# Moving four weight buffers by 128 bytes inside on-chip memory

## The reference, cut to what matters

```
proj = h @ w_in[l]
gates = jax.nn.sigmoid((h @ w_gate[l]).reshape(B, S, N_BRANCHES, D) + b_gate[l])
mixed = jnp.sum(gates * up, axis=2) @ w_out[l]
m = jnp.square(jax.nn.relu(h @ w_up[l])) @ w_down[l]
...
p = h @ w_l
return (g_a * y_a + g_b * y_b) @ w_o
```

## Time and profile before

| What | Value |
|---|---|
| median of three runs | 2254.39 us |
| profiled execution | 2254.39 us |
| its span | 2252.6 us |
| TensorE busy | 2216.8 us, 98% |
| VectorE busy | 1510.1 us, 67% |
| ScalarE busy | 1071.6 us, 48% |
| GpSimd busy | 121.5 us, 5% |
| granted TensorE clock, mean | 0.996 |
| HBM read | 468.09 MB, 210 GB/s over the span |

### The profile page before, as it was taken

The page is one execution under the profiler, slowest core; times in us unless marked ns, Lnnn a source line. Parts: engine busy times, 40 slices in busy tenths (PEclk is TensorE's granted clock), DMA queues, the critical chain, the costliest instruction groups (busy, mean ns, idle before and its releaser), DMA issues.

```text
span 2252.6 us, 37367 instructions
## 1 busy us (share of the span) xinstructions
PE 2216.8 (98%) x15836; PEld 2065.2 (92%) x15836; DVE 1510.1 (67%) x1864; ACT 1071.6 (48%) x1422; POOL 121.5 (5%) x81
## 2 busy tenths in 40 slices
PE   7999999999999999999999999999999999999998
PEld 7889999999999888988988998998889989999986
DVE  6867588899989767554555554555766555678655
ACT  5444435554444456544443443444656545444443
POOL 1100010111100201000000000000100000011000
PEclk9999999999999999999999999999999999999999
DMA  8855667677787665656656656656754545788763
GB/s 279 240 179 163 201 211 247 218 237 254 240 267 245 236 227 178 191 196 191 196 193 195 192 194 196 201 194 204 246 173 147 157 135 165 245 295 292 254 215 139
DMA packets 246382, 474.73 MB, mean 211 GB/s; under 512 B 21054, under 2 KB 25512, under 8 KB 244424
## 3 DMA queue, kind: packets, MB, share of 16 engines
q1 hardware_dynamic: 242888, 454.40, 63.0%
q0 software_dynamic: 3328, 17.96, 2.3%
HBM read 468.09 MB, written 4.21 MB: 210 GB/s over the span
## 4 chain that ended last, share of the span: by engine, by line
PE 90%; DVE 6%; issue 1%; ACT 1%; POOL 1%; DMA 1%; POOLq 0%; SPq 0%; ACTq 0%; DVEq 0%
PE ps L867 18%; PE ps L869 18%; PE ps L868 18%; PE ps L860 11%; PE ps L862 11%; PE ps L861 11%; DVE wloW L1227 1%; DVE tmp L1255 1%; PE ps L795 1%; DVE tmp L1400 1%; PE ps L651 1%; PE ps L677 1%; ACT whiW L899 1%; POOL tmp L538 0%; PE ps L784 0%
## 5 line engine op out<-in xcount | busy, mean ns | idle before, releaser
L867 PE MATMUL ps<-op0h,whiW 128*128 128x256 f32 x3248 | 907.4, 279 | 7.7 <-DVE wloW L1227 7.7
L869 PE MATMUL ps<-op0h,wloW 128*128 128x256 f32 x3248 | 899.3, 277 | 0.0
L868 PE MATMUL ps<-op0l,whiW 128*128 128x256 f32 x3248 | 899.3, 277 | 0.0
L1227 DVE TENSOR_TENSOR wloW<-raw,whiW 128x1024 fp32r<-128x1024 f32 (+1 forms) x488 | 600.2, 1242 | 339.5 <-ACT whiW L899 337.2
L899 ACT ACTIVATE whiW<-raw 128x1024 fp32r<-128x1024 f32 (+1 forms) x488 | 512.3, 1057 | 569.6 <-PE ps L869 421.6
L867 PEld LDWEIGHTS ps<-op0h,whiW 128*128 128x128 f32 x3248 | 612.1, 188 | 11.5 <-DVE wloW L1227 7.0
L868 PEld LDWEIGHTS ps<-op0l,whiW 128*128 128x128 f32 x3248 | 612.3, 189 | 2.0 <-issue 1.4
L869 PEld LDWEIGHTS ps<-op0h,wloW 128*128 128x128 f32 x3248 | 612.2, 188 | 0.0
L1227 DVE TENSOR_TENSOR wloT<-raw,whiT 128x1024 fp32r<-128x1024 f32 (+1 forms) x280 | 338.3, 1218 | 274.3 <-ACT whiT L899 274.0
L899 ACT ACTIVATE whiT<-raw 128x1024 fp32r<-128x1024 f32 (+1 forms) x280 | 290.8, 1047 | 318.1 <-PE ps L862 257.6
L860 PE MATMUL ps<-whiT,op1h 128*128 128x512 f32 x640 | 249.4, 390 | 0.0
(11 more groups left out here) (260 smaller groups left out, 2178.1 us busy)
## 6 DMA issues: line engine op xcount, KB each, us to landing
raw<-in_w_in SPq DMA_DIRECT2D x256, 512.0 KB, 4.4
raw<-in_w_up SPq DMA_DIRECT2D x128, 512.0 KB, 3.8
raw<-in_w_down SPq DMA_DIRECT2D x128, 512.0 KB, 4.0
raw<-in_w_ada SPq DMA_DIRECT2D x96, 512.0 KB, 5.0
raw<-in_w_gate SPq DMA_DIRECT2D x96, 512.0 KB, 4.9
raw<-in_w_out SPq DMA_DIRECT2D x64, 512.0 KB, 4.4
raw<-in_w_branch SPq DMA_DIRECT2D x48, 512.0 KB, 5.2
raw<-in_w_proj_a SPq DMA_DIRECT2D x24, 512.0 KB, 5.0
```

Of the source, the lines that this page charges most:

```text
L867: pe.matmul(o, wh, xh[:, ka, :], start=first and m % 2 == 0, stop=False, skip_group_check=True)
L868: pe.matmul(o, wh, xl[:, ka, :], start=False, stop=False, skip_group_check=True)
L869: mm = pe.matmul(o, wl, xh[:, ka, :], start=False, stop=last, skip_group_check=True)
L1227: v.tensor_tensor(wlo[job.mode][q % NSPL][:, :, 0:job.n], x, h.bitcast(F32), ALU.subtract).then_inc(s_lo, 1)
```

## The change

`split_buffers` had a second argument, the distance in bytes from a slot's start to its W buffer: 64 for the high parts and 192 for the low parts. It now has none, and 64 holds for both.

```diff
-        def split_buffers(name, stand):
+        def split_buffers(name):
 ...
-                for mode, shift in (("T", 0), ("W", stand)):
+                for mode, shift in (("T", 0), ("W", 64)):
                     w[mode].append(at(f"{name}{mode}{i}", [128, KC, 512], o + shift, F32R))
-                top[0] = o + stand + 4 * KC * 512
+                top[0] = o + 64 + 4 * KC * 512
             return w
 
-        whi, wlo = split_buffers("whi", 64), split_buffers("wlo", 192)
+        whi, wlo = split_buffers("whi"), split_buffers("wlo")
```

## The result

The changed kernel took 2285.2 us, the median of four runs (2280.08 to 2289.41 us), against 2254.52 us for the kernel before (four runs, 2254.38 to 2257.48 us). The recorded ratio of the runs is 1.0132, with a 95% interval of 1.0108 to 1.0155. I had forecast 2254.4 us.

A forecast was written before the change was run, and what follows sets the result against it. The prediction took the kernel to be bound by the pace at which TensorE's matmuls follow one another. Its terms, 2254.39 + 0 + 0 + 0, gave 2254.4 us, with an 8-in-10 range of 2250.3 to 2258.5 us.

The forecast's parts named there:

- The weight loads: Term for TensorE's load of `wloW` in mode W: pace independent of start address, 0 us, bounds -15.2 to +16.3 us.
- Mode T as a witness: Argument that mode T, standing and moving both at remainder 64, keeps the same pace: 226.7 ns, twice 113.3 for twice the columns.
- Rows 10: Profile rows of mode W's slowest stall-free stretch found, 8 matmuls at 117.5 ns each; gave the upper bound, +16.3 us.
- Rival A: Loads sharing a remainder collide, slowing line 868's matmuls from 113.3 towards 117.5 ns: +16.3 us, 2270.7 us; chance 0.04.
- The writes: Term for VectorE's write of `wloW` (line 1227, mode W): address makes no difference, 0 ns a write.
- Rival D: VectorE's writes of `wloW` slower by the full 13 ns, nothing hiding them: 6.2 us, 2260.6 us; chance 0.02.
- Other meetings: Term for engines' steps meeting at other moments, one TensorE wait for `wloW` more or less: 0, range +-3.1 us.
- Rival B: Remainder 0 of `wloW` costs something now; line 868's pace would go towards 109.4 ns: -15.2 us, 2239.2 us; chance 0.04.

The follow-up runs named there:

- one_in_four: Changed kernel with only the fourth of the four `wloW` buffers back at remainder 0 modulo 256: 2261.3 us.
- write0_load128: Changed kernel with `wloW` written by VectorE at remainder 0 as before, still loaded by TensorE at 128 (wrong columns computed): 2288.9 us.
- both64: Changed kernel with `whiW` and `wloW` both at remainder 64, like the activations, instead of 128: 2320.9 us.
- swap: Kernel before with the two remainders exchanged, `whiW` at 0 and `wloW` at 128: 2264.3 us.
- write128_load0: Changed kernel with `wloW` still written by VectorE at remainder 128, but loaded by TensorE at 0 as before (wrong columns computed): 2253.9 us.
- next_slot: Changed kernel with each chunk's low part in the next of the four slots, both parts still at remainder 128: 2286.6 us.
- lo224: Kernel before with `wloW` at remainder 224 instead of 0, `whiW` still at 128: 2298.6 us.
- lo32: Kernel before with `wloW` at remainder 32 instead of 0, `whiW` still at 128: 2292.2 us.

## Why the prediction was wrong

**The weight loads, the step that failed.** I argued that loads with remainders 128, 0 and 64 all went at 113.3 ns, that the trace held 2 x 3888 loads of the kind that `wloW` was to become, and took 0 us. Each of these numbers was right. What failed is the inference that a load's cost is its own. `one_in_four` shows that the pace is a state of the whole stream, and `write0_load128` that the loads alone decide on it: the loads of `whiW` at 128 were fast because the load of `wloW` at 0 between them kept the 117.8 ns pace from lasting. With it gone, all three lines slowed, not only the third of the stream that I had put at stake (440.5 us) and charged nothing. The three kinds of distance have means of 117.0, 117.0 and 116.8 ns, against 113.5 ns each before, and the term is 39.8 us where I had 0.

**Mode T as a witness** failed as well. Standing and moving at one remainder is the best layout there and the worst in mode W (`both64`, 120.0 ns). A matmul of 256 columns beside a load of 128 is not half of one of 512.

**Rows 10 were the state itself.** I used 117.5 ns as an upper bound and left it an oddity. It was the 117.8 ns pace, already in the trace in rows of up to 8, each time close behind a break in the stream. That something ended it was the thing to explain, and the one candidate that differed from its neighbours was the remainder of `wloW`. Rival A had this pace and the right sign, at a chance of 0.04, but charged it to line 868 alone: 16.3 us. All three lines, slow 80% of the time, give 3 x 16.3 x 0.80 = 39.1 us, close to the 39.8 us measured. Its condition, that loads share a remainder, isn't the right one either: in `swap` they don't, and the slow pace lasted for up to 1,126 matmuls. Nor do writes take part.

**The writes** were right. The write's mean went from 1246 to 1257 ns and its idle time from 336.3 to 354.3 us, and `write128_load0` shows that its address has no effect. Rival D is refuted by the same run. The median stayed at 1225 ns. The mean follows the loads and not the write's own address: it is 1243 ns in `write128_load0` and 1256 ns in `write0_load128`. Why a slower stream lengthens some of the writes isn't shown.

**Other meetings** went the way of fewer stalls, 5.3 us in all, outside my +-3.1 us.

**Rival B** asked whether remainder 0 had a cost. It had a use. Its lower end rested on a row of another kind: the transposes of the earlier trace rows move 128 columns each, so 109.4 ns is no faster stream than 113.3 ns for 256. The Trainium skill ("TensorE: Matmul & The Clock Gate", section "Back-to-back issue gap") gives N/2.4 plus 2.5 ns for isolated warm matmuls, by which an estimate for 256 columns is 109.2 ns. The mean of no layout here came down to that; 113.5 ns was the lowest, wherever the operands lay as a whole.

What stays open: what in the memory makes the two paces, why a stretch starts in one or the other (the stretch near 940 us in the changed kernel started fast, of itself), and whether a third operand layout, say with `op0h` and `op0l` at different remainders, is faster than 113.3 ns. None of these was tried. The start of a stretch may well be a matter of chance: with the loads at the same remainders the changed kernel has 9,250 slow distances, `write0_load128` 8,679 and `next_slot` 8,534, and the changed kernel's four times lie 9.3 us apart where those of the kernel before lie 3.1 us apart.

## What to carry to other kernels

- Where TensorE is the bound and weights are loaded beside every matmul, the start addresses of the moving and standing operands, modulo 256 bytes, are a parameter worth up to 3.8% here (2254.5 to 2339.8 us, both modes together). Write them down as such and measure them, all together: moving all of them by 64 or by 32 bytes changed nothing, moving the low part alone by 32 cost 38 to 44 us.
- A uniform pace in a trace doesn't prove that each instruction's cost is its own. Look for the short stretches with another pace, ask what ends them, and whether the change takes that away.
- Read the pace from starts; the page's busy times and durations showed this loss only as 3 ns.

## What the hardware did that I had not expected

- A stream of float32r matmuls with 256 moving columns can run at two lasting paces, 113.3 and 117.8 ns a matmul, with the same instructions and remainders (in the changed kernel for up to 644 and 1,918 distances in a row); where standing and moving operands have one remainder it runs at 120.0 ns. At 2.4 GHz 256 columns are 106.7 ns, so the 113.3 ns pace is 1/16 and the last 1/8 above one column per cycle. In mode T 226.7 ns are 1/16 above 213.3.
- A single weight load at remainder 0 among loads at 128 can switch the slow pace off until the next break in the stream (20 slow rows in `one_in_four` end with one). The reverse, a load at 128 among loads at 0, doesn't do it (`swap`, slow rows of up to 1,126).
- Where VectorE writes has no part in it (2253.9 and 2288.9 us with the write's place exchanged against the load's).
- A distance of 128 bytes matters and one of 256 more doesn't (2285.2 and 2286.6 us, tried in the changed layout alone). A shift of 32 bytes in one operand matters (`lo224`, `lo32`: 2298.6 and 2292.2 us), while a shift of 32 in all does not (2254.4 us).
